# A two-layer decoder block on one core: the values of attention B in two blocks, and the Fourier mixer and first scores partly within a projection

## The chip, the cores and the metric

The kernel runs on one core of one Trainium2 chip. The metric is the device time of one execution in microseconds (us), the median of three runs. The core's engines are TensorE (PE in the profile, with its weight loads as PEld), VectorE (DVE), ScalarE (ACT), GpSimd (POOL) and SyncE (SP); each works through its own instructions in program order and waits on semaphores for the others.

## What is computed

The input is a sequence of 256 tokens of width 1024 in float32. Two mixers with layer norm come first (a sparse attention, then the stick-breaking attention, here attention B), and then a two-layer block: Fourier and neighbourhood mixer, cross attention to a memory, gated feed-forward, and again with a gated convolution. The two places that matter here, cut down:

```python
def stick_breaking_mixer(x, w_in, w_out):            # attention B, 16 heads of 64
    q, k, v, g = split(x @ w_in, 4)
    z = q k^T / 8                                     # per head, 256 x 256
    before = pos_k < pos_q
    log_one_minus = where(before, log_sigmoid(-z), 0)
    log_stick = reverse_cumsum(log_one_minus) - log_one_minus
    a = where(before, exp(log_sigmoid(z) + log_stick), 0)
    return ((a @ v) * silu(g)) @ w_out

def fourier_na_mixer(h, w_in, rpb, w_out):            # h is normalised
    zf, q, k, v = split(h @ w_in)                     # 512 columns each
    yf = real(fft2(zf as [256, 4 groups, 128]))       # over tokens and channels
    ya = softmax(q k^T * scale + bias) @ v            # attention N, 4 heads of 128
    return concat([yf, ya]) @ w_out
```

## The kernel before

Weights come in chunks of 1 MB, each in two halves, streamed by SyncE into four raw slots. ScalarE makes the high part of each half (`hi`, line 1082, raw to `wh`), VectorE the low part (`lo`, line 1586, `wl`), and TensorE multiplies the chunk in three products (high by high, low by high, high by low). `wh` and `wl` have two slots, so the high part of a half waits until TensorE has used the half four places back (`w_used`). The phases (`schedule()`) follow one another in a fixed order written out by hand; a phase takes its PSUM banks from its place in that order, alternating between banks 0, 1 and banks 2, 3, and `enter(p)` makes TensorE wait until the banks of the phase but one before have been read out. A projection "in columns" (`project`, L505 for plain, L511 and L513 for `apart`) gives the transposed result, 48 products of 256 columns to a chunk. A projection "of tokens" (`project_tokens`, L593; `wide=True`) gives tokens by columns, 24 products of 512 columns to a chunk, in groups of six: one group to a half and token tile. `hooks` put other TensorE work behind a named group: key (chunk, half, tile) in `project_tokens`, (chunk, half, k) in `project`.

Attention B. The order is gb (gates), vb (values, 4 chunks), qkb (queries and keys, 8 chunks), attB (no weights), ob (output projection). The heads run as a pipeline of steps t. For a head a, in its order:
- `z_scores(a, a+1)` on TensorE, a pair at once at an odd step (L915, L918), into bank 4 or 5; heads 12 and 13 use two banks of the projection instead (`logit_bank`);
- `z_keep(a)` on VectorE (L1887) adds the mask and copies to SBUF (`z_neg`);
- `z_soft(a)` on ScalarE: Abs, Exp, Ln (L1358, L1360, L1361); `z_sum(a)` on VectorE (L1896), whose result GpSimd splits in two for heads 0 to 9;
- `z_sums(a)` on TensorE at step a+2 (L935, L938 for split heads, L941, L942 for heads 10 to 15), into bank 6 + a % 2, once `z_argument(a-2)` has read that bank;
- `z_argument(a)` on VectorE at step a+3 (L1903); it writes a ring of four tiles, so it waits until the values of head a-4 have been multiplied;
- `z_exp(a)` on ScalarE at step a+4 (L1366);
- `z_values(a, a+1)` on TensorE at an even step a+6 (L958, L960, L962), then `gated` on VectorE (L1750) and a split by GpSimd (L2163, L2165).

Steps 0 to 10 (`B_EARLY` = 11) lie in qkb as hooks, one to a half chunk. Steps 11 to 20 follow behind qkb with no projection around them ("the tail").

The mixer stage. The order is zf (2 chunks), qn, kn, vn (2 chunks each), fourier, attN, oab. After vn, TensorE issues the scores of heads 0 and 1 of attention N (L709), then for each Fourier group g `f_tokens(g)` (L1008), ScalarE's copy (L1419, here "sums out"), `f_channels(g)` (L1018, L1019), ScalarE's copy (L1425, "mixed"), VectorE's join (L1965 to L1967), ScalarE's high part (L1429, "joined high") and VectorE's low part (L1971, "joined low"). Attention N follows: scores of heads 2 and 3, softmax (`logits` L1713 and `normalise` L1721, L1725 on VectorE; `exponentials` L1180 on ScalarE), transposes on TensorE (`turn_probs`, L742), ScalarE's copy of them (`turned_out`, L1189), values on TensorE (L760, L761), ScalarE's and VectorE's parts of the result (L1439, L1762). The output projection oab may start on the Fourier groups and heads 0 and 1 (tiles 0 to 5) and needs heads 2 and 3 for its tiles 6 and 7.

Of the kernel before, what the change touches and what calls it, by code (L numbers as in the profile page):

```python
# [19 lines left out]
F32 = mybir.dt.float32  # L20
# [54 lines left out]
def schedule():  # L75
# [93 lines left out]

TOKBASE = bases(("qi", 1), ("qa", 2), ("ka", 2), ("va", 2), ("vb", 2), ("zf", 1), ("vn", 1), ("vx0", 2), ("vx1", 2), ("fd1", 2))  # L170

# [25 lines left out]
def build(nc, w, xt, memt, vecs, cst, wkw, dft, rpb, gain, out):  # L197
    ctx = ExitStack()
    with ctx:
# [117 lines left out]

        FIRST_HALF, B_EARLY = 5, 11

# [139 lines left out]
        def _(pe):  # L459
# [285 lines left out]
            def soft_attention(name, heads, value_ops, group, p, values_in):  # L745
# [48 lines left out]
                for t in range(2, heads + sums):  # L794
                    if t < heads:
# [149 lines left out]
            def z_values(a):  # L945

                if a == 0:
                    pe.wait_ge(act_evac, PH["vb"].end)
                pe.wait_ge(z_prob, a + 2)
# [13 lines left out]

            project_tokens("vb", xh, xl)

# [27 lines left out]
            project("kn", xx)  # L993
            project_tokens("vn", xh, xl)
            pe.wait_ge(dve_evac, PH["kn"].end)
            for a in range(2):
                scores("N", a)
            pe.wait_ge(act_evac, PH["zf"].end)
            pe.wait_ge(dft_in, 16)
            pf = PH["fourier"]  # L1000
            enter(pf)

            def f_tokens(g):

                if g >= 2:
# [14 lines left out]

            for g in range(5):
                if g < 4:
                    f_tokens(g)
                if g >= 1:
                    f_channels(g - 1)
            pn = PH["attN"]
# [41 lines left out]
        def _(act):  # L1068
# [122 lines left out]
            def soft_attention(name, heads, high, lag, start=1):  # L1191

                copies = depth(name)[1]
                for t in range(start, heads + lag):
                    if copies <= t < heads + copies:
                        turned_out(name, t - copies)
                    if t < heads:
                        exponentials(name, t)
                    high(t)
# [145 lines left out]
            act.activation(ones_r[:, :], ones[:, :], ACT.Copy).then_inc(tri_ready, 1)  # L1345
            chunks("vb", v_copy)

# [26 lines left out]
            def queries_keys(c, b):  # L1374
# [11 lines left out]
            hi(2 * pb.n0 + 2)  # L1386

# [21 lines left out]
            chunks("kn", low=kt)  # L1409
            chunks("vn", scaled_tokens(v), hold=True)  # L1410
            for t in range(2):
                exponentials("N", t)
            pf = PH["fourier"]
            for g in range(6):
                if g < 4:
                    act.wait_ge(f_full, g + 1)
                    if g >= 2:
                        act.wait_ge(o_full, OBASE["F"] + g - 1)
                    act.activation(wk(8 + g % 2)[:, 0:S], bank[6 + g % 2][:, 0:S], ACT.Copy).then_inc(f_copied, 1)  # L1419
                if 1 <= g < 5:  # L1420
                    a = g - 1
                    act.wait_ge(o_full, OBASE["F"] + a + 1)
                    if a >= 2:
                        act.wait_ge(f_joined, a - 1)
                    act.activation(f_sums(a), bank[pf.pair + a % 2][:, 0:S], ACT.Copy).then_inc(f_mixed, 1)  # L1425
                if g >= 2:
                    a = g - 2
                    act.wait_ge(f_joined, a + 1)
                    act.activation(yh[:, a, :], f_out(a), ACT.Copy).then_inc(y_hi, 1)  # L1429

# [139 lines left out]
        def _(dve):  # L1570
# [304 lines left out]
            chunks("gb", gates_summed)  # L1875
            chunks("vb")

# [28 lines left out]
            def z_step(t):  # L1906
                if B_EARLY <= t < NH:
# [7 lines left out]
            chunks("qkb", hold=True, ahead=in_order({divmod(FIRST_HALF + t, 2): [(z_keep, t)] for t in range(B_EARLY)}),  # L1915
                   after=in_order({divmod(FIRST_HALF + t, 2): [(z_step, t)] for t in range(B_EARLY)}))
            for t in range(B_EARLY, NH + 6):
                z_step(t)
            lo(2 * PH["attB"].n0 + 2)
            residual("ob", None, None, ALPHA)  # L1920
# [28 lines left out]
            chunks("kn", times_rb(kt, low="kn"))  # L1949
            chunks("vn", hold=True)  # L1950
            dve.wait_ge(bias_ready, 8)
            for a in range(2):
                logits("N", a, nabias_of(a), NA_SCALE)
            for a in range(2):
                normalise("N", a)
            pf = PH["fourier"]
            for g in range(5):
                if g < 4:

                    dve.wait_ge(f_mixed, g + 1)  # L1960
                    if g >= 2:
                        dve.wait_ge(y_hi, YBASE["F"] + g - 1)
                        dve.wait_ge(dve_evac, pf.base + g - 1)
                    e, o, y = f_sums(g)[:, EVEN], f_sums(g)[:, ODD], f_out(g)
                    dve.tensor_tensor(y[:, 1:P], e[:, 1:P], o, ALU.add)  # L1965
                    dve.tensor_tensor(y[:, S - 1:P:-1], e[:, 1:P], o, ALU.subtract)
                    dve.tensor_copy(y[:, 0:P + 1:P], e[:, 0:P + 1:P]).then_inc(f_joined, 1)  # L1967
                if g >= 1:
                    a = g - 1
                    dve.wait_ge(y_hi, YBASE["F"] + a + 1)  # L1970
                    dve.tensor_tensor(yl[:, a, :], f_out(a), yh[:, a, :].bitcast(F32), ALU.subtract).then_inc(dve_evac, 1)  # L1971
            soft_attention("N", 4, lambda a: nabias_of(a), NA_SCALE, plain_low("N", 1, 4), 4, done=2)
            residual("oab", "xa0", "xa0")
# [388 lines left out]
```

## Time and profile before

| | us |
|---|---|
| median of three runs (991.9 to 992.2) | 991.91 |
| the profiled execution | 991.94 |
| its span | 990.1 |
| PE busy | 973.1 (98%) |
| PEld busy | 880.1 (89%) |
| DVE busy | 688.8 (70%) |
| ACT busy | 556.1 (56%) |
| POOL busy | 203.5 (21%) |

The trace's times count from the start of the span. The time of an execution is the span and 1.84 us around it. A matmul in a float32 product that isn't split shows as two records. Matmuls are pipelined: a row's duration runs to the modelled end of the last, while the next row's start tells when TensorE went on.

### The profile page before, as it was taken

What the parts mean: (1) busy time and instruction counts of PE and PEld (TensorE: products, weight loads), DVE (VectorE), ACT (ScalarE), POOL (GpSimd) and SP (SyncE); (2) the same over time, 40 slices, a digit from 0 to 9 for tenths busy, and PEclk for the clock granted to TensorE, in tenths of its full rate; (3) what the DMA queues carried; (4) which work ended last, traced back from release to release, by engine and by line L of the source; (5) the groups of instructions that cost most, each with busy time, mean ns of one, the idle gap of its engine ahead of it and who ended that gap; (6) DMA issues with size and microseconds to landing.
All of it is one profiled execution on the core that took longest, in us unless ns stands there. A gap on an engine that the chain in (4) does not pass through costs nothing.

```text
span 990.1 us, 16686 instructions
## 1 busy us (share of the span) xinstructions
PE 973.1 (98%) x6532; PEld 880.1 (89%) x6532; DVE 688.8 (70%) x1056; ACT 556.1 (56%) x856; POOL 203.5 (21%) x193
## 2 busy tenths in 40 slices
PE   9999989999999999999999999999999999999997
PEld 8779759988997988798899899999898989989985
DVE  5789785854567687555556779776787665767973
ACT  5556673664676374655355456554455555546662
POOL 0002034300243450012003005220044301202610
PEclk9999999999999999999999999999999999999999
DMA  9634525465432537346414655557546432555431
GB/s 364 240 135 163 176 88 206 166 216 213 170 129 89 182 129 263 118 170 212 143 71 169 213 180 185 187 188 282 191 170 251 162 140 94 196 183 182 173 151 43
DMA packets 24831, 172.93 MB, mean 175 GB/s; under 512 B 2752, under 2 KB 2880, under 8 KB 4416
## 3 DMA queue, kind: packets, MB, share of 16 engines
q1 hardware_dynamic: 23040, 160.66, 45.5%
q10 hardware_dynamic: 1728, 11.40, 3.0%
q8 instruction: 42, 0.69, 0.3%
q14 instruction: 21, 0.17, 0.1%
HBM read 166.81 MB, written 5.24 MB: 174 GB/s over the span
## 4 chain that ended last, share of the span: by engine, by line
PE 92%; ACT 2%; DVE 2%; issue 1%; DMA 1%; POOL 0%; SPq 0%; ACTq 0%; DVEq 0%
PE banks L505 37%; PE banks L593 16%; PE banks L511 14%; PE banks L513 7%; PE banks L503 6%; PE banks L655 4%; PE banks L709 1%; DMA raw<-w 1%; PE banks L760 1%; PE banks L761 1%; DVE work L1713 1%; PE banks L742 1%; PE banks L833 0%; DVE work L1725 0%; ACT work L1180 0%
## 5 line engine op out<-in xcount | busy, mean ns | idle before, releaser
L1586 DVE TENSOR_TENSOR wl<-raw,wh 128x1024 fp32r<-128x1024 f32 x300 | 379.8, 1276 | 157.5 <-ACT wh L1082 156.0
L1082 ACT ACTIVATE wh<-raw 128x1024 fp32r<-128x1024 f32 x300 | 313.2, 1054 | 184.7 <-PE banks L505 76.1
L511 PE MATMUL banks<-xx,wh 128*128 128x512 f32 x544 | 192.5, 398 | 0.0
L505 PE MATMUL banks<-xx,wh 128*128 128x256 f32 x1024 | 190.3, 285 | 0.0
L505 PE MATMUL banks<-yy,wh 128*128 128x256 f32 x1024 | 187.8, 285 | 0.1
L505 PEld LDWEIGHTS banks<-xx,wh 128*128 128x128 f32 x1024 | 161.4, 192 | 1.4 <-issue 0.5
L505 PEld LDWEIGHTS banks<-yy,wh 128*128 128x128 f32 x1024 | 160.5, 192 | 0.7 <-issue 0.5
L513 PE MATMUL banks<-xx,wl 128*128 128x256 f32 x544 | 151.4, 278 | 0.0
L505 PE MATMUL banks<-xx,wl 128*128 128x256 f32 x512 | 144.8, 283 | 0.0
L505 PE MATMUL banks<-yy,wl 128*128 128x256 f32 x512 | 138.6, 283 | 0.0
L511 PEld LDWEIGHTS banks<-xx,wh 128*128 128x128 f32 x544 | 102.0, 188 | 23.0
L593 PE MATMUL banks<-wh,xx 128*128 128x512 f32 x352 | 111.3, 397 | 0.8 <-ACT wh L1082 0.5
L513 PEld LDWEIGHTS banks<-xx,wl 128*128 128x128 f32 x544 | 102.5, 188 | 0.3
L505 PEld LDWEIGHTS banks<-yy,wl 128*128 128x128 f32 x512 | 98.2, 192 | 0.2
L505 PEld LDWEIGHTS banks<-xx,wl 128*128 128x128 f32 x512 | 98.1, 192 | 0.1
L593 PEld LDWEIGHTS banks<-wh,xx 128*128 128x128 f32 x352 | 65.7, 188 | 16.6 <-issue 2.9
L593 PE MATMUL banks<-wl,xx 128*128 128x512 f32 x176 | 64.8, 390 | 0.0
L2171 POOL TENSOR_TENSOR work<-work,qz 128x512 f32<-128x512 f32 x18 | 29.3, 1627 | 134.2 <-ACT work L1501 133.0
L2134 POOL TENSOR_TENSOR acc<-work 128x256 f32<-128x256 f32 x9 | 9.2, 1027 | 201.1 <-ACT work L1131 201.1
L1139 ACT ACTIVATE xx<-h,vec 128x256 fp32r<-128x256 f32 x48 | 21.8, 502 | 43.9 <-DVE h L1697 32.7
L2137 POOL TENSOR_TENSOR acc<-acc,work 128x256 f32<-128x256 f32 x27 | 29.9, 1107 | 71.4 <-ACT work L1131 70.4
L1938 DVE TENSOR_TENSOR qz<-banks,qz 128x512 f32<-128x512 f32 x30 | 20.7, 690 | 29.3 <-ACT qz L1099 25.0
(221 smaller groups left out, 1447.2 us busy)
## 6 DMA issues: line engine op xcount, KB each, us to landing
raw<-w SPq DMA_DIRECT2D x149, 1024.0 KB, 4.8
m_scratch<-yy ACTq DMA_DIRECT2D x2, 1024.0 KB, 6.2
k_scratch<-kt ACTq DMA_DIRECT2D x2, 1024.0 KB, 8.3
kt<-k_scratch ACTq DMA_DIRECT2D x2, 1024.0 KB, 6.0
yy<-m_scratch ACTq DMA_DIRECT2D x2, 1024.0 KB, 5.8
raw<-w SPq DMA_DIRECT2D x2, 512.0 KB, 5.3
h<-xt SPq DMA_DIRECT2D x2, 512.0 KB, 6.1
v<-memt ACTq DMA_DIRECT2D x1, 1024.0 KB, 7.7
```

Of the source, the lines that this page charges most:

```text
L503: return pe.matmul(b[:, j, at], weights, o_[:, kk, :], start=k0 + k == 0 and q == 0, stop=k0 + k == KT * p.deep - 1 and q == 2, skip_group ...
L505: return pe.matmul(b[:, j, :], weights, o_[:, kk, :], start=k0 + k == 0 and q == 0 and (j == 0 or not both_open), stop=k0 + k == KT * p.de ...
L511: pe.matmul(b[:, j, :], wh[:, slot, j, k * P:k * P + P], operand[:, :, tile0 + k0 + k, :], start=k0 + k == 0, stop=False, skip_group_check ...
L513: return pe.matmul(b[:, j, 0:S], wl[:, slot, j, k * P:k * P + P], oh[:, tile0 + k0 + k, :], start=False, stop=k0 + k == KT * p.deep - 1, s ...
L593: mm = pe.matmul(bank[p.pair + t][:, :], (oh, oh, ol)[q][:, tile0 + k, t * P:t * P + P], (wh, wl, wh)[q][:, slot, half, e * 2 * CW:(e + 1) ...
L655: mm = pe.matmul(bank[(p.pair ^ 2 * block) + t][:, :], (yh, yh, yl)[q][:, k, t * P:t * P + P], (wh, wl, wh)[q][:, slot, half, e * 2 * CW:( ...
L1082: act.activation(wh[:, n % 2, j, :], raw[:, n % RAW_SLOTS, j, :], ACT.Copy).then_inc(hi_ready, 1)
L1139: ins = act.activation(xh[:, m, :], h[:, m, :], ACT.Copy, scale=vc(gain, m))
L1586: dve.tensor_tensor(wl[:, n % 2, j, :], raw[:, n % RAW_SLOTS, j, :], wh[:, n % 2, j, :].bitcast(F32), ALU.subtract).then_inc(lo_ready, 1)
L1938: chain(dve.tensor_tensor(d, b[0], d, ALU.add))
L2137: chain(pool.tensor_tensor(acc[:, :], acc[:, :], part[:, 0, :], ALU.add))
L2171: pool.tensor_tensor(wk3(7 + c % 2), a, b, ALU.mult).then_inc(pf_ready, 1)
```

## The change

1. Phase vb becomes vb0 (2 chunks, heads 0 to 7) ahead of qkb and vb1 (2 chunks, heads 8 to 15) behind attB; the weights are reordered on the host to match. An empty phase turnB keeps the banks of ob.
2. Steps 11 to 14 of attention B become hooks in vb1 (`B_LOOP` = 15); steps 15 to 20 remain as the tail. `z_values(8)`, which needs the values of vb1, moves from step 14 to step 15, behind `z_sums(13)`. The scores of heads 12 and 13 use banks 4 and 5 like the others and wait for `z_keep` of heads 10 and 11. The held half of the weights moves from the last chunk of qkb to the last of vb1.
3. In the mixer stage, the scores of heads 0 and 1 and `f_tokens` of groups 0 and 1 become hooks in vn; VectorE's logits 0 and 1 and ScalarE's exponentials 0 and 1 and first two copies move into vn with them.
4. Behind vn, the scores, logits and exponentials of heads 2 and 3 are put between the Fourier groups instead of behind them, on all three engines; the transposes and values of attention N come after all of it, as before.

```diff
-    add("vb", 4, "act", wide=True)
+    add("vb0", 2, "act", wide=True)
     add("qkb", 8, "act")
     add("attB", 0, "dve", 8)
+    add("vb1", 2, "act", wide=True)
+    add("turnB", 0, "dve", 0)
...
-        FIRST_HALF, B_EARLY = 5, 11
+        FIRST_HALF, B_EARLY, B_LOOP = 5, 11, 15
...
-            if name == "B" and a in (12, 13):
-                return bank[PH["qkb"].pair + a % 2]
...
-                if heads[0] in (12, 13):
-                    pe.wait_ge(act_evac, PH["qkb"].end)
-                elif heads[0] >= 2:
-                    pe.wait_ge(z_neg, 12 if heads[0] == 14 else heads[-1] - 1)
+                if heads[0] >= 2:
+                    pe.wait_ge(z_neg, heads[-1] - 1)
...
             project("qkb", xx, hooks=hooks)
-            for t in range(B_EARLY, NH + 5):
+            hooks = {}
+            for t in range(B_EARLY, B_LOOP):
+                at = divmod(t - B_EARLY, 2)
+                if t % 2:
+                    hooks[at + (0,)] = lambda t=t: z_scores(t + 1, t + 2)
+                elif t - 6 < NH // 2:
+                    hooks[at + (0,)] = lambda t=t: z_values(t - 6)
+                hooks[at + (1,)] = lambda t=t: z_sums(t - 2)
+            project_tokens("vb1", xh, xl, hooks=hooks)
+            for t in range(B_LOOP, NH + 5):
                 if t < NH + 2:
                     z_sums(t - 2)
-                if t % 2 and t + 1 < NH:
-                    z_scores(t + 1, t + 2)
+                if t == B_LOOP:
+                    z_values(8)
                 if t % 2 == 0:
                     z_values(t - 6)
...
(TensorE, mixer stage)
+            project_tokens("vn", xh, xl, hooks={
+                (0, 1, 1): first_scores_n, (1, 0, 0): lambda: scores("N", 1), (1, 0, 1): lambda: f_tokens(0),
+                (1, 1, 0): lambda: f_tokens(1)})
+            enter(pf)
+            f_channels(0)
+            f_tokens(2)
+            scores("N", 2)
+            f_channels(1)
+            f_tokens(3)
+            scores("N", 3)
+            f_channels(2)
+            f_channels(3)
...
(ScalarE, attention B)
-            chunks("qkb", queries_keys, hold=True,
+            chunks("qkb", queries_keys,
                    between={divmod(FIRST_HALF + t, 2): lambda t=t: z_step(t) for t in range(B_EARLY)})
-            for t in range(B_EARLY, NH + 4):
+            chunks("vb1", lambda c, t, b: v_copy(1, t, b), hold=True,
+                   between={divmod(t - B_EARLY, 2): lambda t=t: z_step(t) for t in range(B_EARLY, B_LOOP)})
+            for t in range(B_LOOP, NH + 4):
                 z_step(t)
...
(ScalarE, mixer stage)
+            def before_values():
+                exponentials("N", 0)
+                sums_out(0)
+                exponentials("N", 1)
+                sums_out(1)
+
+            chunks("vn", scaled_tokens(v), hold=True, between={(1, 1): before_values})
+            mixed(0)
+            sums_out(2)
+            mixed(1)
+            sums_out(3)
+            joined_high(0)
+            exponentials("N", 2)
+            mixed(2)
+            joined_high(1)
+            exponentials("N", 3)
+            mixed(3)
+            joined_high(2)
+            joined_high(3)
...
(VectorE, attention B)
+            chunks("vb1", hold=True, ahead=in_order({divmod(t - B_EARLY, 2): [(z_keep, t)] for t in range(B_EARLY, B_LOOP)}),
+                   after=in_order({divmod(t - B_EARLY, 2): [(z_step, t)] for t in range(B_EARLY, B_LOOP)}))
...
(VectorE, mixer stage)
+            chunks("vn", hold=True, after=in_order({(1, 0): [(logits_n, 0), (logits_n, 1)]}))
+            normalise("N", 0)
+            join(0)
+            normalise("N", 1)
+            logits_n(2)
+            join(1)
+            joined_low(0)
+            logits_n(3)
+            join(2)
+            joined_low(1)
+            normalise("N", 2)
+            join(3)
+            joined_low(2)
+            joined_low(3)
+            soft_attention("N", 4, lambda a: nabias_of(a), NA_SCALE, plain_low("N", 1, 4), 4, start=4)
...
(host, order of the weights)
+    vb = wide(wb, 2 * D, 3 * D)
+    chunks += cols(wb, 3 * D, 4 * D) + vb[0:2]
+    chunks += [a for qk in zip(cols(wb, 0, D), cols(wb, D, 2 * D)) for a in qk] + vb[2:4] + cols(x["w_out_b"][0], 0, D) + cols(kv[1], 0, D)
```

## Rows read from the trace of the kernel before

**Rows 1.** The page: busy time of the engines; the chain by engine.
```profile
PE 973.1 (98%) x6532; PEld 880.1 (89%) x6532; DVE 688.8 (70%) x1056; ACT 556.1 (56%) x856; POOL 203.5 (21%) x193
PE 92%; ACT 2%; DVE 2%; issue 1%; DMA 1%; POOL 0%; SPq 0%; ACTq 0%; DVEq 0%
```

**Rows 2.** Windows: stretch, its length, busy PE, PEld, DVE, ACT, POOL; granted clock, DMA.
```profile
298.50:313.40 14.90, 13.03 (x106) 9.20 (x104) 10.82 (x21) 12.73 (x26) 5.07 (x10) 1.00 0.00 1
406.80:424.10 17.30, 15.34 (x82) 12.29 (x81) 11.00 (x47) 12.11 (x36) 0.00 (x0) 1.00 0.07 31
```

**Rows 3.** Timeline, TensorE, a pair of scores within qkb: start, us, instruction.
```profile
275.40 0.28 PE L505 MATMUL banks<-xx,wh 128*128 128x256 f32 x1
275.61 0.70 PE L918 MATMUL banks<-qz,kt 64*128 64x256 f32 x4
...
276.47 0.39 PE L505 MATMUL banks<-xx,wh 128*128 128x256 f32 x1
```

**Rows 4.** Timeline, TensorE, from the end of qkb to ob; in brackets idle and releaser.
```profile
298.46 0.52 PE L935 MATMUL banks<-sp_parts,tri_r 128*128 128x384 f32 x2
...
299.40 0.70 PE L918 MATMUL banks<-qz,kt 64*128 64x256 f32 x4 [0.25 <-ACT kt L1250]
...
301.32 0.44 PE L958 MATMUL banks<-qz,v 128*64 128x128 f32 x4
...
302.13 0.91 PE L941 MATMUL banks<-work,cs 128*128 128x384 f32 x2
...
303.19 0.70 PE L918 MATMUL banks<-qz,kt 64*128 64x256 f32 x4
...
312.60 0.44 PE L958 MATMUL banks<-qz,v 128*64 128x128 f32 x4 [0.39 <-ACT qz L1366]
...
313.40 0.39 PE L505 MATMUL banks<-yy,wh 128*128 128x256 f32 x1
```

**Rows 5.** Timeline, VectorE, the last steps of B.
```profile
308.56 1.13 DVE L1896 SCALAR_TENSOR_TENSOR work<-work 128x384 f32<-128x384 f32 x1 [0.57 <-ACT work L1361]
...
311.44 0.55 DVE L1903 TENSOR_TENSOR qz<-work,banks 128x384 f32<-128x384 f32 x1 [0.49 <-PE banks L942]
```

**Rows 6.** The chain of waits, in order of time: start, us, what; vn's two chunks.
```profile
396.03 10.91 PE banks L593 x48
```

**Rows 7.** Timeline, TensorE, Fourier groups and attention N.
```profile
406.77 1.89 PE L709 MATMUL banks<-kt,qz 128*128 128x256 f32 x8
408.50 1.89 PE L1008 MATMUL banks<-gt,qz 128*128 128x256 f32 x8
...
412.22 0.39 PE L1018 MATMUL banks<-work,gt 128*128 128x129 f32 x2
...
412.67 1.03 PE L1008 MATMUL banks<-gt,qz 128*128 128x256 f32 x4
...
419.47 0.66 PE L742 MATMUL banks<-cs,work 128*128 128x128 f32 x4 [1.10 <-DVE work L1725]
...
423.11 0.67 PE L760 MATMUL banks<-work,v 128*128 128x256 f32 x2 [0.37 <-DVE yy L1762]
```

**Rows 8.** Timeline, ScalarE, two Fourier copies and the first transpose's copy.
```profile
412.87 0.38 ACT L1425 ACTIVATE work<-banks 128x256 f32<-128x256 f32 x1
413.14 0.41 ACT L1429 ACTIVATE yy<-work 128x256 fp32r<-128x256 f32 x1
...
416.55 0.58 ACT L1189 ACTIVATE work<-banks 128x512 f32<-128x512 f32 x1
```

**Rows 9.** The chain of waits, in order of time: exponentials of heads 0 and 1.
```profile
408.41 2.08 ACT work L1180 x8
```

**Rows 10.** Timeline, VectorE, one join of a Fourier group, first and last instruction.
```profile
413.28 0.29 DVE L1965 TENSOR_TENSOR work<-work 128x127 f32<-128x127 f32 x1 [0.74 <-ACT work L1425]
...
413.69 0.16 DVE L1967 COPY work<-work 128x2 f32<-128x2 f32 x1
```

**Rows 11.** One line's instructions, min/median/max ns: the warm-up products at the start.
```profile
L815 PE MATMUL banks<-ones x32: 275/421/579, 1.0 to 6.8; 128*128 128x128 f32 x32
```

More of the change, by code:

```diff
@@ L165, in bases @@
     return table
-TOKBASE = bases(("qi", 1), ("qa", 2), ("ka", 2), ("va", 2), ("vb", 2), ("zf", 1), ("vn", 1), ("vx0", 2), ("vx1", 2), ("fd1", 2))
+TOKBASE = bases(("qi", 1), ("qa", 2), ("ka", 2), ("va", 2), ("vb0", 1), ("vb1", 1), ("zf", 1), ("vn", 1), ("vx0", 2), ("vx1", 2), ("fd1", 2))
 XBASE = bases(*[(u, 4) for u in ("first", "B", "mix0", "xa0", "ffn0", "mix1", "xa1", "ffn1")])
@@ L794, in soft_attention @@
                 for t in range(2, heads + sums):
-                    if t < heads:
+                    if t < heads and name != "N":
                         scores(name, t)
@@ L945, in z_values @@
             def z_values(a):
-                if a == 0:
-                    pe.wait_ge(act_evac, PH["vb"].end)
+                if a in (0, 8):
+                    pe.wait_ge(act_evac, PH["vb1" if a else "vb0"].end)
                 pe.wait_ge(z_prob, a + 2)
@@ L993, in _ @@
             project("kn", xx)
[L994 to L999, printed above, removed]
             pf = PH["fourier"]
-            enter(pf)
             def f_tokens(g):
+                if g == 0:
+                    pe.wait_ge(act_evac, PH["zf"].end)
+                    pe.wait_ge(dft_in, 16)
                 if g >= 2:
@@ L1019, in f_channels, with first_scores_n @@
                 pe.matmul(b[:, ODD], dft_c[:, P:S], wk(8 + g % 2)[:, ODD], start=True, stop=True).then_inc(o_full, 1)
[L1021 to L1025, printed above, removed]
+            def first_scores_n():
+                pe.wait_ge(dve_evac, PH["kn"].end)
+                scores("N", 0)
+            project_tokens("vn", xh, xl, hooks={
[10 more added lines that the diff above has]
+            f_channels(3)
             pn = PH["attN"]
@@ L1196, in soft_attention @@
                         turned_out(name, t - copies)
-                    if t < heads:
+                    if t < heads and name != "N":
                         exponentials(name, t)
@@ L1345, in _ @@
             act.activation(ones_r[:, :], ones[:, :], ACT.Copy).then_inc(tri_ready, 1)
-            chunks("vb", v_copy)
+            chunks("vb0", v_copy)
             ZW = S + P
@@ L1409, in _, with sums_out, mixed, joined_high @@
             chunks("kn", low=kt)
-            chunks("vn", scaled_tokens(v), hold=True)
-            for t in range(2):
-                exponentials("N", t)
             pf = PH["fourier"]
[L1414 to L1425, printed above, removed]
-                if g >= 2:
-                    a = g - 2
-                    act.wait_ge(f_joined, a + 1)
-                    act.activation(yh[:, a, :], f_out(a), ACT.Copy).then_inc(y_hi, 1)
+            def sums_out(g):
+                act.wait_ge(f_full, g + 1)
+                if g >= 2:
+                    act.wait_ge(o_full, OBASE["F"] + g - 1)
+                act.activation(wk(8 + g % 2)[:, 0:S], bank[6 + g % 2][:, 0:S], ACT.Copy).then_inc(f_copied, 1)
+            def mixed(a):
+                act.wait_ge(o_full, OBASE["F"] + a + 1)
+                if a >= 2:
+                    act.wait_ge(f_joined, a - 1)
+                act.activation(f_sums(a), bank[pf.pair + a % 2][:, 0:S], ACT.Copy).then_inc(f_mixed, 1)
+            def joined_high(a):
+                act.wait_ge(f_joined, a + 1)
+                act.activation(yh[:, a, :], f_out(a), ACT.Copy).then_inc(y_hi, 1)
+            def before_values():
[16 more added lines that the diff above has]
+            joined_high(3)
             def plain_high(name, heads, tiles, first):
@@ L1875, in _ @@
             chunks("gb", gates_summed)
-            chunks("vb")
+            chunks("vb0")
             ZW = S + P
@@ L1913, in z_step @@
                 zgate(t)
-            chunks("qkb", hold=True, ahead=in_order({divmod(FIRST_HALF + t, 2): [(z_keep, t)] for t in range(B_EARLY)}),
+            chunks("qkb", ahead=in_order({divmod(FIRST_HALF + t, 2): [(z_keep, t)] for t in range(B_EARLY)}),
                    after=in_order({divmod(FIRST_HALF + t, 2): [(z_step, t)] for t in range(B_EARLY)}))
-            for t in range(B_EARLY, NH + 6):
+            chunks("vb1", hold=True, ahead=in_order({divmod(t - B_EARLY, 2): [(z_keep, t)] for t in range(B_EARLY, B_LOOP)}),
+                   after=in_order({divmod(t - B_EARLY, 2): [(z_step, t)] for t in range(B_EARLY, B_LOOP)}))
+            for t in range(B_LOOP, NH + 6):
                 z_step(t)
-            lo(2 * PH["attB"].n0 + 2)
+            lo(2 * PH["turnB"].n0 + 2)
             residual("ob", None, None, ALPHA)
@@ L1949, in _, with logits_n @@
             chunks("kn", times_rb(kt, low="kn"))
-            chunks("vn", hold=True)
-            dve.wait_ge(bias_ready, 8)
-            for a in range(2):
+            def logits_n(a):
+                if a == 0:
+                    dve.wait_ge(bias_ready, 8)
                 logits("N", a, nabias_of(a), NA_SCALE)
-            for a in range(2):
-                normalise("N", a)
+            chunks("vn", hold=True, after=in_order({(1, 0): [(logits_n, 0), (logits_n, 1)]}))
             pf = PH["fourier"]
[L1957 to L1971, printed above, removed]
@@ L1972, in _, with join @@
-            soft_attention("N", 4, lambda a: nabias_of(a), NA_SCALE, plain_low("N", 1, 4), 4, done=2)
+            def join(g):
+                dve.wait_ge(f_mixed, g + 1)
+                if g >= 2:
+                    dve.wait_ge(y_hi, YBASE["F"] + g - 1)
+                    dve.wait_ge(dve_evac, pf.base + g - 1)
+                e, o, y = f_sums(g)[:, EVEN], f_sums(g)[:, ODD], f_out(g)
+                dve.tensor_tensor(y[:, 1:P], e[:, 1:P], o, ALU.add)
+                dve.tensor_tensor(y[:, S - 1:P:-1], e[:, 1:P], o, ALU.subtract)
+                dve.tensor_copy(y[:, 0:P + 1:P], e[:, 0:P + 1:P]).then_inc(f_joined, 1)
@@ L2312 @@
     chunks += cols(x["w_out_a"][0], 0, D) + cols(kv[0], 0, D)
-    chunks += cols(wb, 3 * D, 4 * D) + wide(wb, 2 * D, 3 * D)
-    chunks += [a for qk in zip(cols(wb, 0, D), cols(wb, D, 2 * D)) for a in qk] + cols(x["w_out_b"][0], 0, D) + cols(kv[1], 0, D)
+    vb = wide(wb, 2 * D, 3 * D)
+    chunks += cols(wb, 3 * D, 4 * D) + vb[0:2]
+    chunks += [a for qk in zip(cols(wb, 0, D), cols(wb, D, 2 * D)) for a in qk] + vb[2:4] + cols(x["w_out_b"][0], 0, D) + cols(kv[1], 0, D)
     wn = x["w_in_ab_2"][0]
```

9 lines of the change are left out of this document (6 added, 3 removed).

## The prediction, made before the change was run

> **What bounds the kernel now.** I read the page first: TensorE is busy for 973 of 990 us and holds 92% of the chain of waits [rows 1]. The weights set it, and the change takes none of them away, so a gain can only come out of TensorE's idle time in the two stages touched. Windows over them come next: 14.9 us of tail behind qkb with 13.0 busy, 17.3 us from vn to oab with 15.3 busy, both at a granted clock of 1.00, the 2.4 GHz level [rows 2]. Since modelled ends flatter the busy share, I count by starts in the timeline.
>
> Prices of TensorE's work, from one start to the next: a pair of values 302.13 - 301.32 = 0.81, sums of an unsplit head 303.19 - 302.13 = 1.06 [rows 4]; a pair of scores 276.47 - 275.61 = 0.86, and 0.09 more to get into it from a projection, where spacing by 0.12 would have put its start at 275.52 [rows 3]. The split sums of head 9 take 0.53, estimated from the two halves of the row at 298.46. The tail holds split sums of head 9, six unsplit sums, two pairs of scores, five pairs of values: 0.53 + 6.36 + 1.72 + 4.05 = 12.66 of 313.40 - 298.46 = 14.94 us [rows 4]. Idle: 2.3 us.
>
> In the mixer stage a head's scores take 0.87 (1.73 for two, 406.77 to 408.50), a group's `f_tokens` the same by its equal row, `f_channels` 0.45 (412.22 to 412.67), four transposes 0.44 and a head's values 0.88 (my readings of rows 7 less the pipelined end of each). Four of each make 14.0 of the 17.3 us between 406.77 and oab at 424.05, which is 0.94 behind the start at 423.11. Idle: 3.2 us. Both stages emptied of idle would be worth 5.5 us, 0.55%.
>
> **Attention B, step by step.** I keep the old times and align at the end of qkb, 298.46; the two chunks of vb1 then shift the old start of ob from 313.40 to 324.30, since two wide chunks take 10.9 us [rows 6], eight groups of 1.36.
>
> First, a wait comes in. `enter(vb1)` asks for the last read-out of qkb, whose banks it takes. Before, the split sums of head 9 lay over that wait, and the scores behind them went on at 299.40 [rows 4]. Now those sums are a hook within vb1, so nothing covers it: vb1 starts at 299.40, 0.94 idle. Queued behind on TensorE is everything; no other engine is short of work by it.
>
> Within vb1 (10.9) the hooks are two pairs of scores (0.95 each), values of heads 6 and 7 (0.90), split sums (0.53), sums of heads 10 and 11 (1.06 each), and the sums of head 12 behind its last group (1.06). A step is then 3.3 to 4.7 us long; ScalarE has one high part and four activations to do in it, some 3 us (an estimate: it did four activations and little else per step in the old tail, 12.7 busy for the 5 and a half steps there, 2.3 each [rows 2], and a high part is twice such a row), VectorE less, so I find every hook's input ready: the scores of 12 and 13 come at 300.8 and `z_keep(11)` is due at about 297.6, those of 14 and 15 at 309.6 against `z_keep(13)` at about 307.0. These engines' work is hidden by TensorE's 1.36 us groups; uncovered, one late hook would cost up to 1 us. Weights: the half once held is now made in time for vb1, and the raw slots, whose DMAs are idle in the tail (share 0.00) [rows 2], load ahead as before, so SP's and the weight queue's order costs nothing. vb1 and its hooks end at 299.40 + 10.90 + 6.50 = 316.80.
>
> The tail from there: sums of 13 to 317.86; values 8 and 9 to 318.67. Their v was read out behind the last group (315.7 plus about 0.8; a copy of this size takes 0.58) [rows 8], covered by the sums of 12 and 13. Now the moved step bites. `z_argument(12)` overwrites a tile that the values of head 8 read; before, they came a step earlier. It can start at about 318.70, takes 0.55 as the row at 311.44 does [rows 5], and `z_sums(14)`, which needs its bank, waits until 319.30: 0.63 idle. It ends at 320.34, values 10 and 11 at 321.15, sums of 15 at 322.21, values 12 and 13 at 323.02. From the end of the sums of 15 (322.3) runs argument, exponential, values: before, from 311.44 to 312.60, 1.16 [rows 4, 5], so the last values start at 323.43, with 0.41 idle, and take 0.80 (312.60 to 313.40). ob starts at 324.23 against 324.30: a gain of 0.1 us. The 2.3 us of idle go, and 0.94 + 0.29 (entering hooks) + 0.63 + 0.41 = 2.3 come.
>
> Of one price the sum isn't sure. `z_sum(15)` took 1.13 us where GpSimd was at work beside it, twice the 0.55 of the equally large row at 311.44 [rows 5]; if it does again at 319.5, `z_argument(13)` is done at 321.1, just ahead of the sums of 15 at 321.15. So it costs 0 in place and 0.6 at most where the chain has no room. The Trainium skill ("SBUF — State Buffer", Who interferes with whom) says that a VectorE instruction with two SBUF inputs and a GpSimd one that reads SBUF exclude each other, and whichever is issued first has the port for all its length. By it `z_sum(15)`, queued directly behind `gated`, would go first and take its short time, and GpSimd would wait. No run here has shown that order yet.
>
> Bounds for B: if the arguments and exponentials are all hidden, entry and hooks remain (1.2), a gain of 1.1; if one late hook and the port both come in, a loss of 1.5. I take 0.1, nearest to the rows chained.
>
> **The mixer stage.** Moving 2 x 0.87 of scores and 2 x 0.87 of `f_tokens` into vn, where TensorE was already full, moves the end of vn from 406.77 to 410.24, the very time at which they were done before. They were never idle time. What the cover buys is that ScalarE's copies 0 and 1 are ready, so `f_channels(0)` runs at 410.24 rather than with the idle time behind 410.23 (0.6). Then TensorE has no wait until `turn_probs(1)`: the four channels 0 to 3, tokens 2 and 3, scores 2 and 3, transposes 0 and 1 are 1.80 + 1.74 + 1.74 + 0.88 = 6.16, so it is at 416.4.
>
> Now ScalarE. Its queue holds, behind vn, twelve pieces ahead of `turned_out(0)`, and its order binds. A copy frees it after 0.27 [rows 8], a head's exponentials after 1.0 [rows 9], four instructions of the eight. `sums_out(3)` waits for `f_tokens(3)` and starts at 413.94; then joined high 0 (414.22), exponentials of head 2 (414.50 to 415.48), mixed 2, joined high 1 (free at 416.1), exponentials of head 3 (which also wait for the transpose of head 0, to free its tile, 416.15 to 417.13), mixed 3 (done 417.51), joined high 2 meanwhile, VectorE's join 3 (0.03 + 413.85 - 413.28 = 0.60) [rows 10] to 418.11, joined high 3 (418.14), and `turned_out(0)` at 418.45 to 418.55. Before, it started at 416.55 [rows 8]. So TensorE, ready for the values of head 0 at 416.4, waits until 419.1: 2.7 us where the longest wait before was the 1.10 ahead of 419.47 [rows 7]. Behind it are queued transpose 2, values 1, and all of oab.
>
> From 419.1: values 0 (to 420.0), transpose 2, values 1 (421.3), transpose 3 (421.8). ScalarE copies transpose 2 only now (to 421.2), then the high part of head 0; VectorE's low part frees the bank at 422.0, values 2 go to 422.95; likewise transpose 3's copy (422.5), high and low part of head 1 (423.3 to 423.4), and values 3 start at 423.4 against 423.11 before [rows 7]. oab starts 0.3 us later, at 424.35. The weight halves for it are made as early as before, the held one 0.3 later with 5 us to spare. VectorE has normalised head 2 by 417.6 and head 3 by 419.8, both ahead of their transposes.
>
> Bounds: if `turned_out(0)` came where the copies allow (416.6), the stage would end 1.9 earlier less bank waits of about 0.6 that then bind, 1.3 off the loss of 0.3 and so a gain of 1.0; if each small start costs ScalarE 0.05 more and the joins collide once, a loss of 1.2. I take a loss of 0.3.
>
> **Sum.** 991.94 (span 990.1 and 1.84 around it) - 0.1 + 0.3 = 992.1, and the profiled execution is 0.03 over the median of 991.91, so 992.1 on either.
>
> **Rivals.**
> The idle time goes. The hooks give ScalarE and VectorE 10.9 us of cover twice; for it speaks that four of ten tail steps no longer run bare and that exponentials 0 and 1 vanish from the path [rows 9]. Against it: the tail of B keeps its bare last steps, and TensorE's moved work was no idle. With B at its bound of 1.1 and three quarters of the mixer's 3.2 gone, 991.9 - 3.5 = 988.4; to pass the 2 us below it needs the transposes' copies not queued behind the Fourier ones.
>
> The cross waits multiply. One mechanism on the slow side: each pair of values is awaited by an argument, this by the next sums, and late `z_values` repeat the 0.63 at every pair; with one late normalise at the 1.10 of the row at 419.47, B loses 3 x 0.63 and the mixer 1.1 + 0.3: 991.9 + 3.3 = 995.2. It decides once sums of 15 are late too, that is from `z_argument(13)` over 0.1 us late on. Against it: in my chain only the first pair shows it.
>
> The clock falls. The 2.7 us wait is longer than any TensorE wait in these stages before, and no row of it shows the granted clock off 1.00. If it fell to the 1.2 GHz level, work would stretch as the start hints, where a product has a median of 421 ns and a least of 275 [rows 11]: half as long again or double on the 3.5 us of values and transposes and the head of oab, 3 to 4 us, 995.6. The Trainium skill ("TensorE: Matmul & The Clock Gate", HAM oscillation) puts the fall at longer pauses than this one, and by it the time stays 992.1; that is why the clock has so small a chance.
>
> **How the numbers follow.** What this kernel's measurement tells from no change is about 0.2%, 2 us. The forecast case (both stages within 1.5 us of where they were, netting 992.1) has 0.82, the first rival 0.08, the second 0.06, the clock 0.04. In the forecast case the sum lies between 991.94 - 1.3 and + 1.8; reaching a little into the rivals gives 990.5 to 993.8. Faster is the first rival, 0.08; slower the other two, 0.10; same 0.82.
>
> **What would show it.** In the changed trace: vb1's first product idles about 0.9 behind ScalarE's read-out of kt; the sums of head 14 wait about 0.6 for a `z_argument`; a last wait of 0.4 ahead of the values of 14 and 15. In the mixer stage vn's last product ends where `f_tokens(1)` did, and one wait of about 2.7 us stands ahead of the first values of N, released by the transposes' copy on ScalarE. If that wait is under 1.5 us or the one at vb1 missing, my order of ScalarE is wrong; if hooks show idle before them, the cover is.

## The result and the profile after

| | us |
|---|---|
| changed kernel, median of 20 runs | 993.89 (992.37 to 994.68) |
| kernel before, median of 20 runs | 991.98 (991.58 to 992.52) |
| ratio, 95% interval | 1.0016 (1.001 to 1.0021) |
| profiled execution after | 994.25, span 992.5 |

The change makes the kernel 0.16% slower, which is within the 0.2% that I called no change, though the interval lies wholly above 1, so the loss is real. The median is 0.09 above my range's end of 993.8. The median hides a shape that nobody forecast: 9 of the 20 runs lie between 992.4 and 993.0 and 11 between 993.8 and 994.7, with nothing between. The runs of before lie within 0.94 of each other. The mean granted clock of a whole execution is 0.998 or 0.999 in each of the 9 and 0.996 or 0.997 in each of the 11. The profiled execution is of the upper group; no trace of the lower one was kept.

The page's busy times and chain by engine, after; they answer to [rows 1]:

```profile
PE 974.4 (98%) x6532; PEld 881.7 (89%) x6532; DVE 686.5 (69%) x1056; ACT 556.0 (56%) x856; POOL 205.5 (21%) x193
PE 94%; DVE 2%; ACT 2%; DMA 1%; issue 1%; POOL 0%; SPq 0%; ACTq 0%; DVEq 0%
```

PE is busy 1.3 us more with the same 6532 instructions, so the same work took longer. Windows over the two stages, with the columns of [rows 2]: first attention B from the end of qkb to ob, then the mixer stage behind vn in three parts.

```profile
287.60:313.50 25.90, 24.02 (x154) 17.73 (x152) 14.28 (x26) 17.27 (x31) 5.64 (x11) 1.00 0.24 82
...
416.40:419.30 2.90, 0.31 (x3) 0.07 (x1) 2.67 (x13) 2.57 (x9) 0.00 (x0) 1.00 0.00 0
419.30:423.50 4.20, 4.14 (x15) 3.40 (x16) 1.03 (x3) 1.27 (x3) 0.00 (x0) 0.59 0.00 0
423.50:427.00 3.50, 2.85 (x18) 2.33 (x17) 0.86 (x3) 1.72 (x5) 0.00 (x0) 1.00 0.02 5
```

Attention B takes what it took. In the mixer stage TensorE stands still for 2.64 of the 2.9 us of the second window, and in the 4.2 us behind that its granted clock is 0.59 on the mean, mostly the 1.2 GHz level. The timeline of TensorE there, which answers to [rows 7] (start, us, instruction, idle before and releaser):

```profile
415.68 1.04 PE L743 MATMUL banks<-cs,work 128*128 128x128 f32 x8
419.36 0.85 PE L761 MATMUL banks<-work,v 128*128 128x256 f32 x2 [2.64 <-ACT work L1204]
420.00 1.06 PE L762 MATMUL banks<-work,v 128*128 128x256 f32 x2
420.85 1.06 PE L743 MATMUL banks<-cs,work 128*128 128x128 f32 x4
421.71 1.06 PE L761 MATMUL banks<-work,v 128*128 128x256 f32 x2
422.56 0.88 PE L762 MATMUL banks<-work,v 128*128 128x256 f32 x2
423.27 0.60 PE L743 MATMUL banks<-cs,work 128*128 128x128 f32 x4
...
425.39 0.67 PE L761 MATMUL banks<-work,v 128*128 128x256 f32 x2 [0.65 <-DVE yy L1797]
```

The reader is to see the spacing: four transposes take 0.86 from 420.85 to 421.71, and 0.44 from 423.27 on; between them the clock comes back. The 2.64 us ahead is the wait for ScalarE's copy of the first transpose, whose queue answers to [rows 8]:

```profile
417.31 0.36 ACT L1440 ACTIVATE work<-banks 128x256 f32<-128x256 f32 x1
417.58 0.40 ACT L1444 ACTIVATE yy<-work 128x256 fp32r<-128x256 f32 x1
418.31 0.42 ACT L1444 ACTIVATE yy<-work 128x256 fp32r<-128x256 f32 x1 [0.33 <-DVE work L2004]
418.63 1.07 ACT L1204 ACTIVATE work<-banks 128x512 f32<-128x512 f32 x2
```

And attention B on TensorE, which answers to [rows 4]; all of it came 10.9 us earlier until vb1, since two chunks of the values now lie behind it:

```profile
288.44 0.50 PE L594 MATMUL banks<-wh,xx 128*128 128x512 f32 x1 [0.69 <-ACT kt L1265]
...
306.86 0.44 PE L957 MATMUL banks<-work,v 128*64 128x128 f32 x4
...
308.54 0.88 PE L940 MATMUL banks<-work,cs 128*128 128x384 f32 x2 [0.80 <-DVE work L1938]
...
312.71 0.44 PE L957 MATMUL banks<-qz,v 128*64 128x128 f32 x4 [0.40 <-ACT qz L1381]
...
313.52 0.39 PE L506 MATMUL banks<-yy,wh 128*128 128x256 f32 x1
```

ob starts at 313.52 against 313.40.

### The profile page after: what moved, and what is told of

Same layout as the page of the kernel before. It is cut to its first block, busy times and chain, and to the rows that moved or that the text cites. A ratio compares the mean times of both kernels' runs of the same rounds, so it can differ in the third digit from the quotient of the medians.

```text
span 992.5 us, 16687 instructions
## 1 busy us (share of the span) xinstructions
PE 974.4 (98%) x6532; PEld 881.7 (89%) x6532; DVE 686.5 (69%) x1056; ACT 556.0 (56%) x856; POOL 205.5 (21%) x193
## 4 chain that ended last, share of the span: by engine, by line
PE 94%; DVE 2%; ACT 2%; DMA 1%; issue 1%; POOL 0%; SPq 0%; ACTq 0%; DVEq 0%
PE banks L506 37%; PE banks L594 16%; PE banks L512 14%; PE banks L514 7%; PE banks L504 6%; PE banks L656 4%; PE banks L710 1%; DMA raw<-w 1%; PE banks L761 1%; PE banks L762 1%; PE banks L743 1%; PE banks L917 1%; DVE work L1748 0%; PE banks L834 0%; DVE work L1760 0%
## 5 line engine op out<-in xcount | busy, mean ns | idle before, releaser
L594 PE MATMUL banks<-wh,xx 128*128 128x512 f32 x352 | 114.6, 402 | 1.2 <-ACT kt L1265 0.7
```

The lines of the kernel that those rows point to most:

```text
L594: mm = pe.matmul(bank[p.pair + t][:, :], (oh, oh, ol)[q][:, tile0 + k, t * P:t * P + P], (wh, wl, wh)[q][:, slot, half, e * 2 * CW:(e + 1) ...
```

## The experiments

The theory from the two traces: B is neutral; the mixer's order makes a 2.6 us wait; behind it the clock falls in some executions and not in others, and the executions in which it falls are the upper group. Each kernel below was timed against the kernel before on the same chip (its median there was 991.88, 992.03 or 991.92).

**1. One part alone.** Two kernels: B's parts of the diff only, and the mixer's parts only.

> Only attention B's part of the change (vb0, vb1, steps 11 to 14 as hooks), the mixer stage as before. Theory (the loss is in the mixer stage: a 2.6 us wait of TensorE ahead of the first values of N, and a granted clock that falls behind it in about half of the executions): B adds 0.1 us, so 992.1, all runs within 0.5 us of each other, and the granted clock stays at 1.00 from 400 to 430 us. Rival (the moved values cost the 1.9 us, through the wait at the start of vb1 and the late values of heads 8 and 9): 993.5 to 994, with the changed kernel's two groups of times.

> Only the mixer stage's part of the change, attention B as before. Theory: the whole loss, 992.4 in the executions in which the clock holds and 994.1 in those in which it falls, both occurring; TensorE waits 2.6 us for ScalarE's copy of the first transpose. Rival (B costs it): 992.0 in all runs.

B alone: 992.06 (991.62 to 992.36, 11 runs), ratio 1.0001 (0.9992 to 1.001), one group. The mixer alone: 993.86 (992.3 to 994.34), ratio 1.0016 (1.0007 to 1.0025), 3 runs at 992.3 to 992.7 with a mean clock of 0.999 and 8 from 993.6 up with 0.996 or 0.997. So the loss is the mixer's, and the two groups too. Windows of the mixer-only kernel:

```profile
416.40:419.30 2.90, 0.30 (x3) 0.07 (x1) 2.67 (x13) 2.57 (x9) 0.00 (x0) 0.92 0.00 0
419.30:422.00 2.70, 2.65 (x8) 2.22 (x9) 0.60 (x2) 0.39 (x1) 0.00 (x0) 0.50 0.00 0
```

Here the clock is at 0.50, the 1.2 GHz level, for all of the 2.7 us behind the wait, and it went down within the wait (a mean of 0.92 over it).

**2. The order of ScalarE's queue.** The changed kernel, with one move:

```diff
             joined_high(1)
+            turned_out("N", 0)
+            turned_out("N", 1)
             exponentials("N", 3)
...
-            soft_attention("N", 4, plain_high("N", 4, 1, 4), 4, start=2)
+            soft_attention("N", 4, plain_high("N", 4, 1, 4), 4, start=4)
```

> The changed kernel with ScalarE copying the first two transposes of N (turned_out 0 and 1) right behind joined_high(1), ahead of the exponentials of head 3 and the rest of the Fourier group 3. Theory (the order of ScalarE's queue makes the wait, the wait drops the clock): the wait ahead of the first values falls from 2.6 to about 0.3 us, the clock stays at 1.00, one group of times; head 3's normalising comes later, so another wait of about 1.5 us appears ahead of its transpose, and the time is 991.7 to 992.5. Rival (the clock falls for a reason other than this wait, such as float32 products or transposes as such): two groups of times remain.

Measured 991.81 (991.59 to 991.89, 11 runs), ratio 0.9999 (0.999 to 1.0008): one group. TensorE's timeline:

```profile
417.11 0.67 PE L761 MATMUL banks<-work,v 128*128 128x256 f32 x2 [0.34 <-ACT work L1204]
...
420.99 0.66 PE L743 MATMUL banks<-cs,work 128*128 128x128 f32 x4 [1.48 <-DVE work L1762]
```

The wait is 0.34 instead of 2.64, and the later 1.48 us wait, which comes because ScalarE now does head 3's exponentials later, leaves the clock alone. Two copies in another place took away 2.1 us of median. This run changes the wait and the queue's order together; the next two keep the order.

**3. The wait kept, TensorE at work in it.** Eleven products of which nothing is used ("fillers"), then five, behind the two transposes; the diff shows the eleven; ScalarE's queue as in the changed kernel.

```diff
                     if t == sums:
                         enter(p)
                         pe.wait_ge(act_evac, PH[values_in].end)
+                        if name == "N":
+                            pe.wait_ge(s_read, 2 * (u0 + 2) + 2)
+                            for _ in range(11):
+                                pe.matmul(bank[4][:, 0:P], ones[:, :], ones[:, :], start=True, stop=True)
```

> The changed kernel with 11 extra products of ones by ones (128 columns, float32, 0.22 us each, 2.4 us in all, result unused) issued on TensorE behind the two transposes, in the wait ahead of the first values. Nothing else moves: ScalarE's copy comes at the same time. Theory (the pause itself drops the clock): no fall, granted clock 1.00 in this stretch, one group of times at 992.4 to 992.7. Rival (queue order alone costs the 1.9 us and the clock is a by-product): 993.9 as the changed kernel. If the fillers only add work, 994 or more.

> The changed kernel with 5 filler products (1.1 us) in place of 11, so that TensorE works until 417.7 and then idles 1.6 us to the first values, as long as the longest wait of the kernel before and of the kernel with the copy first (1.5). Theory (the length of the idle stretch decides): no fall, one group at 992.3 to 992.8. Rival (any stretch with TensorE half idle lets it fall): some executions at 994.

Eleven: 992.5 (992.09 to 992.82), ratio 1.0006 (0.9996 to 1.0015). Five: 992.6 (992.14 to 993.02), ratio 1.0006 (0.9997 to 1.0015). One group each, 11 runs each. The values come at the same time as in the changed kernel:

```profile
416.76 2.62 PE L806 MATMUL banks<-ones 128*128 128x128 f32 x22
419.48 0.70 PE L761 MATMUL banks<-work,v 128*128 128x256 f32 x2
```

```profile
419.39 0.70 PE L761 MATMUL banks<-work,v 128*128 128x256 f32 x2 [1.43 <-ACT work L1208]
...
416.70:419.40 2.70, 1.27 (x13) 1.08 (x11) 2.50 (x12) 2.37 (x9) 0.00 (x0) 1.00 0.00 0
419.40:424.30 4.90, 4.49 (x23) 3.50 (x24) 1.74 (x5) 2.56 (x6) 0.00 (x0) 1.00 0.00 0
```

The first fence is of the kernel with eleven, the second of that with five, with its windows. Adding useless work to TensorE makes the changed kernel 1.3 us (five) or 1.4 us (eleven) faster at the median, to where its own lower group is (its median is 992.61), and no run of either is above 993.02. This separates the two prices: the queue's order costs some 0.5 us (992.61 less the 991.98 of before and the 0.12 of B), the fall some 1.6 (the difference of the two groups' medians).

**4. A longer pause.** Three extra copies on ScalarE ahead of `turned_out(0)`.

```diff
             joined_high(3)
+            for _ in range(3):
+                chain(act.activation(wk(7), c_("adm"), ACT.Copy))
```

> The changed kernel with three extra ScalarE copies of 512 columns (0.5 us each, result unused) ahead of turned_out(0): the wait ahead of the first values grows from 2.6 to about 4.1 us. Theory: the clock falls in every execution; 992.5 + 1.5 for the longer wait + 1.6 for the clock = 995.5 in one group. Rival (the two groups come from something that differs between executions and not from the pause): two groups, at 994.0 and 995.7.

Measured 996.13 (995.73 to 997.52, 5 runs), ratio 1.0041 (1.0028 to 1.0055). The pause was 4.63 us, longer than the 4.1 I meant, since each copy waited for the one before (three took 1.94). By the later start of the values (421.68 for 419.36) a run at full clock would be due near 994.9, an estimate from the lower group's 992.61; all five are above it. The profiled execution is the slowest of them, and the others lie 0.9 or more below it: its mean clock is 0.994, theirs 0.997. The low level holds for all of the 5.8 us behind the pause, and began within it:

```profile
421.68 1.19 PE L761 MATMUL banks<-work,v 128*128 128x256 f32 x2 [4.63 <-ACT work L1204]
...
417.00:421.70 4.70, 0.07 (x2) 0.05 (x1) 3.02 (x12) 4.27 (x12) 0.00 (x0) 0.91 0.00 0
421.70:427.50 5.80, 5.80 (x18) 4.78 (x19) 0.42 (x1) 1.52 (x4) 0.00 (x0) 0.50 0.00 0
```

**5. What TensorE does ahead of the pause.** The two transposes ahead of the last two `f_channels`.

```diff
-                    if turns <= t < heads + turns:
+                    if turns <= t < heads + turns and not (name == "N" and t - turns < 2):
...
             scores("N", 3)
+            pe.wait_ge(f_copied, 4)
+            turn_probs("N", 0)
+            turn_probs("N", 1)
             f_channels(2)
```

> The changed kernel with the two transposes of N ahead of f_channels(2) and (3) instead of behind them: the same work, the same wait of about 2.6 us, but the last TensorE work ahead of it is ordinary products and not transposes. Theory A (only the wait counts): falls in about half of the executions, two groups at 992.4 and 994.1. Theory B (transposes don't count as activity, so in the changed kernel the pause is really 0.9 us longer than TensorE's idle time): fewer or no falls, 992.5.

Measured 994.78 (994.67 to 995.58, 7 runs), ratio 1.0029 (1.0018 to 1.004). It doesn't answer its question cleanly. I had overlooked that `mixed(2)` on ScalarE waits for `f_channels(2)`, now 0.87 later, so the pause grew to 3.21 us. As a point between 2.64 and 4.63 it is of use: by the start of the values a run at full clock would be due near 993.3 (the same estimate), and all seven are above 994.6 with a mean clock of 0.997 or, in one, 0.994. Where the fall lies is new:

```profile
420.09 0.67 PE L761 MATMUL banks<-work,v 128*128 128x256 f32 x2 [3.21 <-ACT work L1207]
...
420.10:421.00 0.90, 0.90 (x4) 0.78 (x5) 0.55 (x2) 0.33 (x1) 0.00 (x0) 1.00 0.00 0
421.00:424.40 3.40, 3.40 (x14) 2.90 (x13) 0.42 (x1) 0.87 (x2) 0.00 (x0) 0.52 0.00 0
```

TensorE was back at work for 0.9 us at full clock before it fell. The last work ahead of this pause was ordinary products, so transposes ahead of it aren't needed for a fall. Nor does the run fit theory B well: without the transposes counted, TensorE's pause in the changed kernel would be 3.7 us (415.68 to 419.36), longer than the 3.21 here, and yet it fell less often. But the pause changed too, so whether transposes count as activity stays open.

**6. B's idle time.** The kernel with B's part only, with one and with both of these moves on TensorE:

```diff
+                if t > B_EARLY:
                     hooks[at + (1,)] = lambda t=t: z_sums(t - 2)
+            z_sums(B_EARLY - 2)
             project_tokens("vb1", xh, xl, hooks=hooks)
             for t in range(B_LOOP, NH + 5):
+                if t == B_LOOP:
+                    z_values(8)
                 if t < NH + 2:
                     z_sums(t - 2)
-                if t == B_LOOP:
-                    z_values(8)
```

> Only B's part of the change, with only the first of its two moves: the split sums of head 9 ahead of vb1. Theory (the wait at the start of vb1 is bare in the changed kernel and costs what lay over it before): 992.05 - 0.5 = 991.5, and the other 0.8 us (wait ahead of the sums of 14) stays. Rival (the gain of 1.3 is all from the earlier values of heads 8 and 9): 992.0.

> The kernel with only attention B's part, and two steps of it moved on TensorE: the split sums of head 9 ahead of vb1 instead of a hook in it (they cover the wait for ScalarE's read-out again, 0.53) and the values of heads 8 and 9 ahead of the sums of head 13 instead of behind them (z_argument(12) comes 1.06 earlier, so the 0.8 us wait ahead of the sums of 14 goes). Theory (my account of B's idle time): 992.0 - 0.5 - 0.7 = 990.8. Rival (the last steps are bound by the chain through ScalarE whatever TensorE does): 991.5 or more.

The first move (`z_sums(9)` ahead of vb1): 991.56 (991.39 to 991.93), ratio 0.9997 (0.9988 to 1.0006), 0.5 under the 992.06 of B alone. Both: 990.72 (990.51 to 991.02), ratio 0.9987 (0.9978 to 0.9996), 0.8 less again. With both, the waits of TensorE from the end of qkb to ob are these two (total, times, longest):

```profile
PE banks L957 <- ACT qz L1376: 0.4, 1, 0.4
PE banks L934 <- POOL sp_parts L2221: 0.2, 1, 0.2
```

The 0.69 and the 0.80 of the changed kernel are gone, the last 0.4 is left, and 0.2 for GpSimd's split of head 9's sums is new.

**7. All of it.** The whole change with B's two moves, ScalarE's two copies early, and head 3 normalised ahead of the last Fourier join:

```diff
             exponentials("N", 3)
-            mixed(3)
             joined_high(2)
-            joined_high(3)
+            mixed(3)
...
(joined_high(3) behind the copy of transpose 2; VectorE:)
             normalise("N", 2)
+            normalise("N", 3)
             join(3)
```

> The whole change with B's two moves (split sums of head 9 ahead of vb1, values 8 and 9 ahead of the sums of 13), with ScalarE's first two transposes' copies behind joined_high(1), and with the normalising of head 3 ahead of the last Fourier join and ScalarE's last joined_high behind the third transpose's copy, so that the 1.5 us wait ahead of head 3's transpose goes. Theory: no TensorE wait over 1.3 us in the mixer stage, clock held, and 991.8 (copy first) - 1.2 (B) - 1.2 (head 3 earlier, less the wait for its bank) = 989.4 in one group. Rival (the end of the mixer stage is bound by the banks of the values, not by head 3's transpose): 990.4 or more.

Measured 990.03 (989.9 to 990.42, 11 runs), ratio 0.9981 (0.9972 to 0.999): the fastest, 1.9 us under before, though 0.6 over what I expected. TensorE's waits in the stage:

```profile
415.79 0.67 PE L761 MATMUL banks<-work,v 128*128 128x256 f32 x2 [0.34 <-ACT work L1206]
...
419.83 0.67 PE L761 MATMUL banks<-work,v 128*128 128x256 f32 x2 [1.16 <-DVE yy L1807]
```

The wait for head 3's transpose turned in part into one for the bank of head 0's values (1.16, released by VectorE's low part of it), which is the mechanism of the rival named there. The time lies between the two that I had named.

## Why the prediction was right or wrong

**What bounds the kernel** held: the two parts tested alone make up the whole. B's adds 0.2 to the median of the kernel before beside it (992.06 for 991.88), the mixer's 0.5 where its clock holds (992.37, the middle of the three lower runs), and the changed kernel's lower group lies 0.6 above. Every sign that I had named for the changed trace is there; none of them was of the clock.

**Attention B** was right in its waits and in sum: +0.12 us where I had -0.1, and 992.06 for the part alone. The wait of `enter(vb1)` is there (the start moved by 0.85 against 0.94; the last product of qkb began at 287.47 and the next was due at 287.59), so is the one ahead of the sums of 14 (0.80 against 0.63) and the last of 0.40 (0.41). The 0.63 was mis-sized because the argument started 0.98 behind the start of the pair of values (307.84 for 306.86), where I had 0.84. That vb1 with its hooks came out right, 17.46 us (288.44 to 305.90) for my 17.40, is in part luck: the hooks took 5.5 and not 6.5, since sums in hooks took 0.79 to 0.86 and not 1.06 and a pair of scores 0.85, while the eight groups around them took 12.0 and not 10.9. Experiment 6 took both the wait at vb1 and the one ahead of the sums of 14 away, and shows their price: 0.5 and 0.8 us.

**The port.** `z_sum(15)` started ahead of GpSimd's cast and took its short 0.55, while the cast took 0.66 where its equals take 0.40. VectorE's row and then GpSimd's, of the changed kernel:

```profile
308.64 0.55 DVE L1931 SCALAR_TENSOR_TENSOR work<-work 128x384 f32<-128x384 f32 x1
...
308.79 0.66 POOL L2214 CAST yy<-work 128x256 fp32r<-128x256 f32 x1 [7.01 <-DVE work L1785]
```

So the cost that I had bounded by 0.6 was 0 here. By the Trainium skill ("SBUF — State Buffer", Who interferes with whom), of two such instructions the one issued first has the port for all its length; this one pair agrees in who was held up.

**The mixer stage.** The mechanism was right, ScalarE's queue and the wait of 2.7 (2.64 measured) at the named place, and so was the remark that the work moved into vn was never idle time. Its price without the fall was too small, 0.3 against about 0.5: the changed kernel's lower group has a median of 992.61, which is 0.63 over before, less 0.12 for B. Experiment 3 gives the same, and shows where: with five fillers the values of head 0 start at 419.39 and those of head 2 at 422.47, which less B's 0.12 is 0.2 and 0.35 later than the 419.1 and 422.0 that I had.

My range was no sum of my bounds: those of the two stages, added up, give 989.8 to 994.6, and I gave no reason for the narrower 990.5 to 993.8. That the median lies so close to its end is no merit, as the range didn't hold the clock at all.

**The step that failed** is the chance of the clock, 0.04. I had its mechanism and its place, and a price of 3 to 4 us. The trace before had no wait of that length on TensorE, which should have left it open; instead I let a page close it. The Trainium skill ("TensorE: Matmul & The Clock Gate", HAM oscillation) puts the fall at longer pauses, and I gave the chance by that. Here the measurement decides: 11 of 20 executions fell behind a 2.64 us pause, and 7 of 7 behind one of 3.21 with ordinary products ahead of it. (If the transposes ahead of the 2.64 us didn't count as work, the first of these would be a pause of 3.7; no run here settles that.) The fall's price was about half of what I had said: the difference of the groups' medians, 994.25 - 992.61 = 1.6. I had stretched 3.5 us of work, but the low level lasted only 3.4 us of time (419.7 to 423.1), which at half speed holds 1.7 us of work and so costs 1.7, an estimate close to the 1.6. The forecast of one time was therefore wrong in form: 992.6 or 994.25, by the execution.

What the pauses did (the pause is that of the profiled execution). The kernels with only B's part have the mixer stage of before, and none of their runs falls:

| kernel | longest TensorE pause in the stage, us | runs in the upper group |
|---|---|---|
| eleven fillers | 0.21 | 0 of 11 |
| before | 1.10 | 0 of 20 |
| all of it tuned | 1.16 | 0 of 11 |
| five fillers | 1.43 | 0 of 11 |
| copy first | 1.48 | 0 of 11 |
| changed | 2.64 | 11 of 20 |
| mixer part only | 2.64 | 8 of 11 |
| transposes early | 3.21 | all 7 |
| three copies more | 4.63 | all 5 |

In the last two no run is near the time due at full clock (993.3 and 994.9, estimates above), and the profile of each shows the fall.

## What to carry to other kernels

Moving work under a projection that already fills TensorE gains nothing by itself (here it paid, 1.9 us, only when the waits that it made were taken away again); what it changes is the order in which the helping engine serves the chain behind, so write out that engine's queue and put the piece that TensorE waits for first. A wait has two prices, its length and what it does to the clock behind it: when a change makes one pause out of several small ones, and the new one is longer than any that the trace shows at full clock, give the fall a real chance. When the runs of one kernel fall in two groups, compare the granted clock by stretches before looking for a cause in the data path.

## What the hardware showed that I had not expected

The clock fell in some executions of one and the same program and not in others at a pause of 2.64 us. Nor did it fall at a fixed time behind TensorE's last work. In two profiles it fell within the pause: 2.1 us after TensorE had stopped with the mixer part only, and 3.8 us after with three copies more. In the other two it fell after the work had begun again: by 0.35 us in the changed kernel, which is 3.0 us after the stop, and by about 1 us with the transposes early, 4.2 us after. The low stretches, of the changed kernel, the mixer part only, the transposes early and the three copies more:

```profile
419.70:423.10 3.40, 3.40 (x12) 2.73 (x11) 0.46 (x2) 0.87 (x2) 0.00 (x0) 0.50 0.00 0
418.90:422.20 3.30, 2.85 (x9) 2.42 (x10) 0.97 (x4) 0.79 (x2) 0.00 (x0) 0.50 0.00 0
421.20:424.50 3.30, 3.30 (x13) 2.83 (x12) 0.42 (x1) 0.87 (x2) 0.00 (x0) 0.50 0.00 0
420.90:427.60 6.70, 5.92 (x18) 4.94 (x19) 0.42 (x1) 2.39 (x6) 0.00 (x0) 0.50 0.00 0
```

Measured in windows of 0.3 us, three of them last 3.4 us and the fourth 6.8, twice as long. By these rows a fall costs about half the length of its low stretch, less what of it lies in the pause (an estimate). The slowest run of the transposes early has the mean clock of that fourth profile (0.994) and may have had a low stretch of its length too; it has no trace.
